# Part of the first modulation vectors computed on TensorE, low parts of the first norm on VectorE, first loads reordered

## The chip, the cores and the metric

One core of a Trainium2 chip runs the whole program. The metric is the device time of one execution in microseconds (us); before the change the median of three runs is 1348.74 us (1347.36 to 1349.37).

## The reference, cut to what matters

The kernel is one inference step of a hybrid encoder layer over 1024 prompt frames and 64 sample frames, model width 1024, all in 32-bit floats. At the start of the layer:

```python
mod = jax.nn.silu(c) @ w_ada + b_ada
sh1, sc1, g1, sh2, sc2, g2 = jnp.split(mod, 6, axis=-1)
h = modulate(rmsnorm(x, ln1), sh1, sc1)        # rmsnorm(x) * g * (1 + sc1) + sh1
rq, rk, rv, rg, aq, ak, av = split_in(h @ w_in)
```

After it come retention and sliding-window attention in four head steps, an output projection, a second norm, a gated MLP with a short convolution, and a final norm. The change touches only what makes `h` and the first products with `w_in`.

## The kernel before, in words

The activations are kept transposed: 8 tiles of 128 model rows (index k) by 1088 frames. Frames are cut into three chunks, c = 0, 1, 2, of 364, 362 and 362 frames; chunk 2 holds the end of the prompt and the sample frames, which have another conditioning vector, so its elementwise operations come in two pieces (298 and 64 frames). A matmul of full accuracy is made as three fp32r passes over a high and a low part of each operand: `act_hl[:, 0]` and `act_hl[:, 1]` for activations, `w_hl` for weights. A high part is written by ScalarE (rounded on the way), a low part is the exact value minus the high part. Weights come in units of 128 output columns; units 0, 1 and 2 are multiplied first.

Every engine runs its own list of instructions in order and waits on semaphores; these lists are written out by hand, and their order is what sets the course of the opening stage:

- SyncE issues the loads in one queue: the conditioning vectors broadcast to all partitions (`silu_c`, 1 MB), modulation tiles of 512 KB (a tile is 128 of the 16x128 scale and shift outputs, outputs on partitions; `load_first_ada`, L495), the three chunks of x (1.4 MB each, `load_x`), weight units, small constants.
- ScalarE applies silu to `silu_c` (L779), squares x (`x_squares`, L755), takes the root of the column sums (`x_root`, L764), splits weights (`split_weights`, L712) and makes high parts, writing the exact value back into a ring of five slots as well (`modulate_x`, L730).
- VectorE multiplies each modulation tile by `silu_c` and sums along the free dimension, once for the prompt and once for the sample (`ada_dots`, L1358, busy on L1368): 14 of the 16 tiles, seven of them ahead of the norm and seven within it. It inverts the roots (`invert`, L1383), adds the bias and makes `scale_n` from a shift and scale pair (`first_vectors(k)`, L1394), and scales x for chunks 1 and 2 (L1425).
- GpSimd multiplies the two other tiles (L1221; ScalarE sums them), multiplies chunk 0 of x by the inverse root (L1230), subtracts the low parts of the weights (L1192) and of all activations (`split_hf`, L1209).
- TensorE sums the squares over partitions with a matrix of ones (L1933, 24 plain fp32 matmuls), then runs the first products k by k: for each k eight groups of three passes, unit u and chunk c, each waiting for the low part of (k, c) (L1963, 192 matmuls). Unit 2 of chunk 2 follows (L1975) with the value transposes between (L1952), and then the head steps (L1918).

Of the kernel before, what the change touches and what calls it, by code (L numbers as in the profile page):

```python
# [19 lines left out]
ALU = mybir.AluOpType  # L20
# [5 lines left out]
P = 128  # L26
# [43 lines left out]
MOD_DVE = (3, 6, 7)  # L70
U_RING = 8
# [33 lines left out]
def hymba_step(nc, x_t, w_units, w_ada, b_ada, cond, gains, conv_wb, conv_st, sinks, ck_t, cv_in, st_in,  # L105
# [4 lines left out]
    with ExitStack() as ctx:  # L110
# [16 lines left out]
        ada_d_phase.close()  # L127
        act_hl = sb("act_hl", [P, 2, KT, T], F32R)
# [91 lines left out]
        X_SQ = [sq[:, 0], sq[:, 1], hf[:, 0], hf[:, 1]]  # L220
        X_SUM_BANK = [0, 1, 2]


        ada_place = [ada_w[:, 0], ada_w[:, 1]] + [t[:, 0:D] for t in (rk, rg, rq, rv, aq)]
        ada_pool_place = [ak[:, 0:D], prob[:].rearrange("p a b c -> p (a b c)")]
# [5 lines left out]
        cond_loaded = sem("cond_loaded")  # L231
        x_loaded = [sem(f"x_loaded{c}") for c in range(3)]
        x_again = [sem(f"x_again{c}") for c in range(3)]
        x_tile_again = sem("x_tile_again")
        ada_loaded = [sem(f"ada_loaded{r}") for r in range(7)]
        ada_pool_loaded = [sem(f"ada_pool_loaded{r}") for r in range(2)]
# [10 lines left out]
        ada_product = sem("ada_product")  # L247
        ada_summed = sem("ada_summed")
# [6 lines left out]
        x_inv_ready = sem("x_inv_ready")  # L255
        x_normed = sem("x_normed")
# [224 lines left out]
        def _(sp):  # L481
# [13 lines left out]
            def load_first_ada(m):  # L495
                if 12 <= m < 14:
                    sp.dma_start(ada_pool_place[m - 12], w_ada[m]).then_inc(ada_pool_loaded[m - 12], 16)
                    return
                nth = ADA_DVE.index(m)
                if nth >= 7:  # L500
                    sp.wait_ge(ada_used, 2 * (nth - 7) + 2)
                sp.dma_start(ada_place[nth % 7], w_ada[m]).then_inc(ada_loaded[nth % 7], 16)
# [25 lines left out]
            load_first_ada(12)  # L528
# [4 lines left out]
            load_first_ada(6)  # L533
            load_unit(1, [1])
            load_unit(2, [2])
            for dst, src in ((b_ada_sb, b_ada), (gains_sb, gains), (ident, ident_in), (conv_wb_sb, conv_wb),
                             (conv_st_sb, conv_st)):
                sp.dma_start(dst[:], src).then_inc(const_loaded, 16)
            for m in (7, 8, 13, 9, 10, 11, 14, 15):
                load_first_ada(m)  # L540
# [163 lines left out]
        def _(act):  # L704
# [25 lines left out]
            def modulate_x(k, c):  # L730

                item = 3 * k + c
                if c == 0:
                    act.wait_ge(vec_ready, k + 1)
                    act.wait_ge(x_normed, k + 1)
                    if item >= 5:
                        act.wait_ge(lo_ready, item - 4)  # L740
                else:
                    act.wait_ge(x_scaled, 2 * k + c)
                for ring in (False, True):
                    for o, tok, m, part in pieces(c):
                        slot = H_RING[item % 5][:, o:o + m]
                        src = xm[:, k, tok:tok + m] if c == 0 else slot
                        ins = act.activation(slot if ring else act_hl[:, 0, k, tok:tok + m], src, ACT.Identity,
                                             bias=mod[:, 2 * k + 1, part:part + 1],
                                             scale=1.0 if c else scale_n[:, 0, k, part:part + 1])
                ins.then_inc(hi_ready, 1)  # L750
# [4 lines left out]
            def x_squares(c):  # L755
                a, n = CHUNKS[c]
                act.wait_ge(x_loaded[c], 16)
                for k in range(KT):
                    item = KT * c + k
                    if item >= 4:  # L760
                        act.wait_ge(sq_used, item - 3)
                    act.activation(X_SQ[item % 4][:, 0:n], xm[:, k, a:a + n], ACT.Square).then_inc(sq_ready, 1)

# [6 lines left out]
            def sum_ada(m):  # L770

                for s in range(2):
                    act.wait_ge(ada_product, 2 * (m - 12) + s + 1)
                    src = ada_pool_place[m - 12] if s else acc[:, 0:D]
                    act.activation(src, src, ACT.Copy, accum_out=mod_part[:, m - 4, s:s + 1]).then_inc(ada_summed, 1)
# [4 lines left out]
            x_squares(0)  # L780
            x_root(0)
            x_squares(1)
            x_root(1)
            x_squares(2)
            split_weights(0, [0])
            x_root(2)
            split_weights(1, [1])
            split_weights(2, [2])
            sum_ada(12)

            act.wait_ge(sq_used, 3 * KT)
            for k in range(KT):
                for c in range(3):
                    modulate_x(k, c)
                if k == 4:
                    sum_ada(13)
# [390 lines left out]
        def _(pool):  # L1187
# [27 lines left out]
            def multiply_ada(m, s):  # L1215

                if s == 0 and m > 12:
                    pool.wait_ge(ada_summed, 2 * (m - 12) - 1)
                pool.wait_ge(ada_pool_loaded[m - 12], 16)
                dst = ada_pool_place[m - 12] if s else acc[:, 0:D]  # L1220
                pool.tensor_tensor(dst, ada_pool_place[m - 12], silu_c[:, s], ALU.mult).then_inc(ada_product, 1)  # L1221

            pool.wait_ge(silu_c_ready, 1)
            for s in range(2):
                multiply_ada(12, s)

            pool.wait_ge(x_inv_ready, 1)
            for k in range(KT):
                x = xm[:, k, 0:CHUNKS[0][1]]
                pool.tensor_tensor(x, x, std[:, 0], ALU.mult).then_inc(x_normed, 1)  # L1230
            for n in range(3):
                split_weights(n, [n])
            for k in range(KT):
                for c in range(3):
                    split_hf(3 * k + c, c, k, H_RING)
                if k in (1, 3):
                    multiply_ada(13, k // 2)
# [106 lines left out]
        def _(dve):  # L1344
# [44 lines left out]
            def first_ada_dots(m):  # L1389

                nth = ADA_DVE.index(m)
                ada_dots(nth, nth // 7 + 1, nth % 7, m % 8 if m < 12 else m - 4)

            def first_vectors(k):  # L1394

                m = 2 * k
                if k < 6:
                    then_wait(add_ada_bias(m, 2, m + 2, m % 8))
                else:
                    dve.wait_ge(ada_summed, 4)  # L1400
                    then_wait(add_ada_bias(m, 2, 12 if k == 6 else len(ADA_DVE), m - 4))
# [3 lines left out]


            dve.wait_ge(silu_c_ready, 1)
            for m in range(7):
                first_ada_dots(m)
                if m in (3, 5):  # L1410
                    invert(m // 2 - 1, m // 2 - 1)
                if m == 3:
                    dve.sem_inc(x_inv_ready, 1)
# [977 lines left out]
```

## Time and profile before

| | us |
|---|---|
| median of 3 runs | 1348.74 |
| the profiled execution | 1349.18 |
| its span, first to last instruction | 1347.4 |
| TensorE busy in it | 1252.2 (93%) |
| VectorE / ScalarE / GpSimd busy | 834.9 / 531.9 / 576.6 |
| mean granted TensorE clock | 0.98 of full |

The profile lists per engine the instructions with start and duration; an operation's duration holds a fixed latency, so that the distance from start to start of a series is what one more operation costs. A granted clock of 1.0 is 2.4 GHz, 0.5 is 1.2 GHz.

### The profile page before, as it was taken

Reading aid. Unit: us, or ns where it says so; the run is one execution under the profiler, and the core shown is the slowest. Engines: PE = TensorE matmul, PEld = TensorE weight load, DVE = VectorE, ACT = ScalarE, POOL = GpSimd, SP = SyncE. Lnnn points to the kernel's source line nnn. Section 1 sums busy time; section 2 is a strip of 40 time slices with the busy share of each in tenths; the row PEclk is TensorE's granted clock in tenths of the full one; section 3 lists DMA queues with packets and bytes.
Section 4 is the critical chain, followed back from the end, with each engine's and each line's share of the span. In section 5 each row is a group of like instructions: output and inputs, shape, how many; then the busy total and the mean of one; then the engine's idle time right before and its main releaser. Section 6 shows DMA issues by size and latency. Waiting matters only on the chain.

```text
span 1347.4 us, 22674 instructions
## 1 busy us (share of the span) xinstructions
PE 1252.2 (93%) x8609; PEld 1193.3 (89%) x8609; DVE 834.9 (62%) x1496; ACT 531.9 (39%) x1074; POOL 576.6 (43%) x351
## 2 busy tenths in 40 slices
PE   5479999999999899778999999999999999999995
PEld 2468898988988899678999999999999999898995
DVE  6966648558376735976566665666656368772305
ACT  5463434344345432444433334333343332424422
POOL 4852113032142342335435344353443577665770
PEclk9799999999999999989999999999999999999998
DMA  9402222223033423212232322323221799595971
GB/s 367 162 35 82 87 73 78 70 88 109 29 115 110 132 68 114 86 45 96 98 113 88 124 97 99 113 88 125 96 99 66 293 353 342 204 334 193 338 257 45
DMA packets 74393, 185.56 MB, mean 138 GB/s; under 512 B 7424, under 2 KB 39744, under 8 KB 74048
## 3 DMA queue, kind: packets, MB, share of 16 engines
q1 hardware_dynamic: 72640, 183.63, 38.0%
q8 instruction: 59, 0.97, 0.3%
q10 hardware_dynamic: 1664, 0.72, 0.2%
q14 instruction: 30, 0.25, 0.1%
HBM read 150.14 MB, written 34.19 MB: 137 GB/s over the span
## 4 chain that ended last, share of the span: by engine, by line
PE 67%; DVE 14%; issue 6%; DMA 5%; POOL 4%; ACT 3%; SPq 0%; DVEq 0%; ACTq 0%; PEldq 0%; POOLq 0%
PE bank L2183 32%; PE bank L1918 13%; PE bank L2223 8%; PE bank L2159 5%; DMA w_raw<-in_w_units 4%; POOL w_more L1331 2%; POOL w_hl L1331 2%; PE bank L2030 2%; DVE ada_out L1368 1%; DVE std L1555 1%; PE bank L2000 1%; PE bank L2015 1%; DMA xm<-in_x_t 1%; PE bank L2064 1%; DVE acc L1825 1%
## 5 line engine op out<-in xcount | busy, mean ns | idle before, releaser
L1918 PE MATMUL bank<-act_hl,w_hl 128*128 128x362 f32 (+1 forms) x1368 | 256.6, 336 | 0.1
L1918 PEld LDWEIGHTS bank<-act_hl,w_hl 128*128 128x128 f32 x1368 | 223.4, 188 | 9.3 <-issue 7.1
L2223 PE MATMUL bank<-u_hl,w_more 128*128 128x362 f32 (+1 forms) x936 | 160.9, 330 | 8.3 <-POOL w_more L1331 7.7
L1192 POOL TENSOR_TENSOR w_hl<-w_raw,w_hl 128x1024 fp32r<-128x1024 f32 x24 | 57.2, 2386 | 260.1 <-ACT w_hl L712 260.1
L2223 PEld LDWEIGHTS bank<-u_hl,w_more 128*128 128x128 f32 x936 | 155.9, 188 | 10.7 <-POOL w_more L1331 9.5
L1331 POOL TENSOR_TENSOR w_more<-w_raw,w_more 128x1024 fp32r<-128x1024 f32 x39 | 109.1, 2816 | 70.9 <-ACT w_more L1093 70.9
L2183 PE MATMUL bank<-x_blocks_b,w_hl 128*128 128x272 f32 x864 | 114.4, 291 | 3.1 <-ACT x_blocks_b L1005 2.0
L2183 PE MATMUL bank<-x_blocks_a,w_hl 128*128 128x272 f32 x864 | 112.9, 289 | 3.9 <-issue 3.9
L2183 PEld LDWEIGHTS bank<-x_blocks_b,w_hl 128*128 128x128 f32 x864 | 111.4, 190 | 4.2 <-ACT x_blocks_b L1005 2.4
L2183 PEld LDWEIGHTS bank<-x_blocks_a,w_hl 128*128 128x128 f32 x864 | 110.4, 189 | 4.4 <-issue 4.3
L2223 PE MATMUL bank<-u_hl,w_hl 128*128 128x362 f32 (+1 forms) x648 | 111.7, 330 | 1.9 <-POOL w_hl L1331 1.9
L2183 PE MATMUL bank<-x_blocks_a,w_ext 128*128 128x272 f32 x840 | 110.1, 290 | 3.6 <-DVE prod_sb L1660 2.4
L2183 PEld LDWEIGHTS bank<-x_blocks_a,w_ext 128*128 128x128 f32 x840 | 107.6, 190 | 4.0 <-issue 2.6
L2223 PEld LDWEIGHTS bank<-u_hl,w_hl 128*128 128x128 f32 x648 | 108.2, 188 | 3.0 <-POOL w_hl L1331 2.5
L2183 PE MATMUL bank<-x_blocks_b,w_ext 128*128 128x272 f32 x840 | 108.3, 287 | 0.0
L2183 PEld LDWEIGHTS bank<-x_blocks_b,w_ext 128*128 128x128 f32 x840 | 106.2, 188 | 0.0
L1295 POOL TENSOR_TENSOR w_ext<-w_raw,w_ext 128x512 fp32r<-128x512 f32 x40 | 53.6, 1349 | 82.5 <-ACT w_ext L982 82.5
L1295 POOL TENSOR_TENSOR w_hl<-w_raw,w_hl 128x512 fp32r<-128x512 f32 x41 | 52.8, 1295 | 79.2 <-ACT w_hl L982 79.2
L1331 POOL TENSOR_TENSOR w_hl<-w_raw,w_hl 128x1024 fp32r<-128x1024 f32 x27 | 73.0, 2719 | 25.7 <-ACT w_hl L1093 25.4
L1093 ACT ACTIVATE w_more<-w_raw 128x1024 fp32r<-128x1024 f32 x39 | 41.3, 1058 | 75.2 <-DMA w_raw<-in_w_units 75.2
L1667 DVE TENSOR_TENSOR up_b<-bank,prod_sb 128x272 f32<-128x272 f32 x44 | 19.4, 441 | 81.2 <-PE bank L2183 81.2
L2159 PE MATMUL bank<-act_hl,w_hl 128*128 128x272 f32 x480 | 64.6, 298 | 4.6 <-POOL w_hl L1288 4.6
(236 smaller groups left out, 2240.7 us busy)
## 6 DMA issues: line engine op xcount, KB each, us to landing
w_raw<-in_w_units SPq DMA_DIRECT2D x142, 512.0 KB, 4.4
ada_w<-in_w_ada_t SPq DMA_DIRECT2D x36, 512.0 KB, 3.7
u_hl<-u_dram SPq DMA_DIRECT2D x44, 362.0 KB, 5.5
u_dram<-acc SPq DMA_DIRECT2D x22, 544.0 KB, 2.7
u_dram<-up_b SPq DMA_DIRECT2D x22, 544.0 KB, 2.7
ada_d<-in_w_ada_t SPq DMA_DIRECT2D x16, 512.0 KB, 5.0
u_hl<-u_dram SPq DMA_DIRECT2D x22, 364.0 KB, 8.2
xm<-in_x_t SPq DMA_DIRECT2D x2, 1448.0 KB, 13.6
```

The costliest lines, as they stand in the source:

```text
L1093: act.activation(w_down(q)[:, 0], w_raw[:, q % 3], ACT.Copy).then_inc(dh_ready, 1)
L1192: pool.tensor_tensor(w_hl[:, slot, 1], w_raw[:, slot], w_hl[:, slot, 0].bitcast(F32), ALU.subtract).then_inc(wl_ready, 1)
L1295: pool.tensor_tensor(w_block(q)[:, 1], a_source(f, i), w_block(q)[:, 0].bitcast(F32), ALU.subtract).then_inc(bl_ready, 1)
L1331: pool.tensor_tensor(w_down(q)[:, 1], w_raw[:, q % 3], w_down(q)[:, 0].bitcast(F32), ALU.subtract).then_inc(dl_ready, 1)
L1368: dve.tensor_tensor_reduce(out, ada_place[place], silu_c[:, s], 1.0, 0.0, ALU.mult, ALU.add, mod_part[:, part, s:s + 1]).then_inc(ada_used, 1)
L1555: dve.reciprocal(std[:, c, 0:n], std[:, c, 0:n]).then_inc(inv_ready, 1)
L1667: ins = dve.tensor_tensor(bb[:, t:t + HC], B[:, 0:HC], gate_sum, ALU.add)
L1918: ins = pe.matmul(bank[c][:, 0:m], w_hl[:, slot, w, k, :], act_hl[:, x, k, a:a + m], start=(pas == 0 and i == 0), stop=(pas == 2 and i == ...
L2030: ins = pe.matmul(bank[6][h, 0:n], av_tok[0:k[1], k[3], h], prob_t[0:k[1], r, g, i, 0:n], start=(i == 0), stop=(i == len(kb) - 1))
L2159: ins = pe.matmul(bank[r % 3][:, 0:HC], w_of[:, w, k, :], act_hl[:, x, k, HC * n:HC * n + HC], start=(pas == i == 0), stop=(pas == 2 and i ...
L2183: ins = pe.matmul(n[:, 0:HC], w_block(q)[:, w, P * k:P * (k + 1)], x_half(h)[:, i, x, k, :], start=(first and pas == k == 0), stop=(pas == ...
L2223: ins = pe.matmul(bank[o][:, 0:m], w_down(q)[:, w, o, :], u_hl[:, q % U_RING, x, 0:m], start=(f == pas == 0), stop=(f == FT - 1 and pas == 2))
```

## The change

Tiles 0 to 9 of the sixteen are no longer multiplied on VectorE (nor 12 and 13 on GpSimd). TensorE transposes each in eight blocks of 128x128 into two PSUM banks, ScalarE copies one bank to SBUF (`w_t`) and VectorE the other, and TensorE multiplies the eight blocks (stationary) by the two columns of `silu_t`, a transposed silu of the conditioning vectors made from a small load. Tiles 10 to 15 stay dots on VectorE, with the old `silu_c`, loaded and activated later. Squares have a buffer of their own, GpSimd adds them in pairs, so TensorE sums 12 arrays in place of 24. VectorE scales all three chunks (GpSimd no longer multiplies chunk 0), ScalarE writes the high part alone, and VectorE makes the low part as (scaled + shift) - high. TensorE starts the first products when the vectors of k = 4 are there. Items (k, c) are taken in a new order, `X_ORDER`.

```diff
+FIRST_COLS = 2 * D + 4 * CHUNKS[0][1] + P + 2 * KT
+PE_ADA = 10
+X_ORDER = ([(0, 0), (1, 0), (2, 0), (0, 1), (1, 1), (2, 1), (3, 0), (3, 1), (0, 2), (1, 2), (2, 2), (3, 2)]
+           + [(k, c) for k in range(4, KT) for c in range(3)])
...
 SP
-            sp.dma_start(silu_c[:, :, :], cond.partition_broadcast(P)).then_inc(cond_loaded, 16)
+            sp.dma_start(ident[:], ident_in).then_inc(ident_loaded, 16)
+            sp.dma_start(cond_rows[0:2 * KT, :], cond.rearrange("s (k p) -> (s k) p", p=P)).then_inc(cond_rows_loaded, 16)
             load_first_ada(0)
             load_first_ada(1)
+            for dst, src in ((b_ada_sb, b_ada), (gains_sb, gains)):
+                sp.dma_start(dst[:], src).then_inc(const_loaded, 16)
             load_x(0)
             load_first_ada(2)
             load_first_ada(3)
             load_x(1)
-            load_first_ada(12)
             load_first_ada(4)
             load_first_ada(5)
             load_x(2)
             load_unit(0, [0])
             load_first_ada(6)
+            load_first_ada(7)
             load_unit(1, [1])
             load_unit(2, [2])
+            load_first_ada(8)
+            load_first_ada(9)
+            sp.dma_start(silu_c[:, :, :], cond.partition_broadcast(P)).then_inc(cond_loaded, 16)
+            for m in range(PE_ADA, 16):
+                load_first_ada(m)
...
 ACT
+            def x_hi_part(k, c):
+                i = X_ORDER.index((k, c))
+                act.wait_ge(x_scaled, i + 1)
+                for o, tok, m, part in pieces(c):
+                    ins = act.activation(act_hl[:, 0, k, tok:tok + m], H_RING[i % 5][:, o:o + m], ACT.Identity,
+                                         bias=mod[:, 2 * k + 1, part:part + 1])
                 ins.then_inc(hi_ready, 1)
...
                     if item >= 4:
-                        act.wait_ge(sq_used, item - 3)
+                        act.wait_ge(sq_used, (item - 4) // 2 + 1)
...
+            def ada_t_copy(t):
+                act.wait_ge(ada_t_done, t + 1)
+                if t >= 2:
+                    act.wait_ge(ada_dot_done, t - 1)
+                act.activation(w_t[:, t % 2, 0:512], bank[2 * (t % 2)][:, :], ACT.Copy).then_inc(ada_t_act, 1)
...
+            act.wait_ge(cond_rows_loaded, 16)
+            act.activation(cond_rows[0:2 * KT, :], cond_rows[0:2 * KT, :], ACT.Silu).then_inc(silu_rows_ready, 1)
+            ada_t_copy(0)
+            ada_t_copy(1)
+            x_squares(0, 0, 8)
+            ada_t_copy(2)
+            ada_t_copy(3)
+            x_root(0)
+            x_hi_part(0, 0)
+            x_hi_part(1, 0)
+            x_squares(1, 0, 4)
+            ada_t_copy(4)
+            x_squares(1, 4, 8)
+            ada_t_copy(5)
+            x_root(1)
+            x_hi_part(2, 0)
+            x_squares(2, 0, 4)
+            for k in range(3):
+                x_hi_part(k, 1)
+            split_weights(0, [0])
+            ada_t_copy(6)
+            x_squares(2, 4, 8)
+            ada_t_copy(7)
+            x_root(2)
+            split_weights(1, [1])
+            x_hi_part(3, 0)
+            x_hi_part(3, 1)
+            split_weights(2, [2])
+            ada_t_copy(8)
+            for k in range(3):
+                x_hi_part(k, 2)
+            ada_t_copy(9)
+            x_hi_part(3, 2)
             act.wait_ge(cond_loaded, 16)
             act.activation(silu_c[:, :, :], silu_c[:, :, :], ACT.Silu).then_inc(silu_c_ready, 1)
+            for k in range(4, KT):
                 for c in range(3):
+                    x_hi_part(k, c)
...
 POOL
+            for p in range(10):
+                add_pair(p)
+            split_weights(0, [0])
+            for p in range(10, 12):
+                add_pair(p)
+            for n in (1, 2):
                 split_weights(n, [n])
-            for k in range(KT):
-                for c in range(3):
-                    split_hf(3 * k + c, c, k, H_RING)
...
 DVE
+            ada_t_copy(0)
+            ada_t_copy(1)
+            first_vectors(0)
+            ada_t_copy(2)
+            ada_t_copy(3)
+            first_vectors(1)
+            invert(0, 0)
+            x_scale((0, 0), (1, 0))
+            x_lo_part((0, 0), (1, 0))
+            ada_t_copy(4)
+            ada_t_copy(5)
+            first_vectors(2)
+            x_scale((2, 0))
+            invert(1, 1)
+            x_lo_part((2, 0))
+            x_scale((0, 1), (1, 1), (2, 1))
+            x_lo_part((0, 1), (1, 1), (2, 1))
+            ada_t_copy(6)
+            ada_t_copy(7)
+            first_vectors(3)
+            x_scale((3, 0), (3, 1))
+            invert(2, 2)
+            x_lo_part((3, 0), (3, 1))
+            x_scale((0, 2), (1, 2), (2, 2))
+            ada_t_copy(8)
+            x_lo_part((0, 2), (1, 2), (2, 2))
+            ada_t_copy(9)
+            x_scale((3, 2))
+            x_lo_part((3, 2))
+            for k in range(4, KT):
+                first_vectors(k)
+                parts = [(k, c) for c in range(3)]
+                x_scale(*parts)
+                if k < KT - 1:
+                    first_ada_dots(2 * k + 2)
+                x_lo_part(*parts)
+                if k < KT - 1:
+                    first_ada_dots(2 * k + 3)
...
 PE
+            def x_sums_of(c, p0, p1):
...
+                if c == 2 and p0 == 0:
+                    pe.wait_ge(std_ready, 1)
+                for p in range(p0, p1):
+                    pe.wait_ge(pair_ready, 4 * c + p + 1)
+                    ins = pe.matmul(bank[X_SUM_BANK[c]][:, 0:n], ones[:, :], x_sq[:, 2 * p % 4, 0:n], start=(p == 0),
+                                    stop=(p == 3))
...
+            ada_transpose(0)
+            ada_transpose(1)
+            ada_dot(0)
+            ada_dot(1)
+            ada_transpose(2)
+            x_sums_of(0, 0, 4)
+            ada_transpose(3)
+            ada_dot(2)
+            ada_dot(3)
+            ada_transpose(4)
+            x_sums_of(1, 0, 2)
+            ada_transpose(5)
+            x_sums_of(1, 2, 4)
+            ada_dot(4)
+            ada_dot(5)
+            x_sums_of(2, 0, 2)
+            ada_transpose(6)
+            ada_transpose(7)
+            x_sums_of(2, 2, 4)
+            ada_dot(6)
+            ada_dot(7)
+            ada_transpose(8)
+            ada_dot(8)
+            ada_transpose(9)
+            ada_dot(9)
+            pe.wait_ge(vec_ready, PE_ADA // 2)
```

## Rows read from the trace of the kernel before

**Rows 1.** The page: two lines of the 40 slices, busy tenths and granted clock.
```profile
PE   5479999999999899778999999999999999999995
...
PEclk9799999999999999989999999999999999999998
```

**Rows 2.** Busy time by stretch: from:to, length, PE, PEld, DVE, ACT, POOL, clock, DMA.
```profile
0.00:46.05 46.05, 17.12 (x48) 9.84 (x49) 34.71 (x35) 23.96 (x41) 26.41 (x20) 0.90 0.98 365
46.05:98.90 52.85, 41.29 (x192) 37.13 (x192) 44.53 (x65) 31.12 (x72) 34.26 (x25) 0.86 0.11 41
...
107.25:1347.40 1240.15, 1187.92 (x8336) 1141.45 (x8336) 753.59 (x1389) 474.48 (x958) 513.60 (x305) 0.99 0.38 134
```

**Rows 3.** The chain that ended last, two pieces of it: start, us, what.
```profile
2.14 10.18 DMA xm<-in_x_t
...
50.42 1.22 DVE ada_out L1368
```

**Rows 4.** Timeline of TensorE, first products: start, us, what, idle before.
```profile
46.05 5.28 PE L1963 MATMUL bank<-act_hl,w_hl 128*128 128x364 f32 x18 [13.66 <-POOL act_hl L1209]
...
62.71 9.47 PE L1963 MATMUL bank<-act_hl,w_hl 128*128 128x364 f32 x42 [3.17 <-POOL act_hl L1209]
...
95.65 3.25 PE L1963 MATMUL bank<-act_hl,w_hl 128*128 128x362 f32 x18 [0.45 <-POOL act_hl L1209]
```

**Rows 5.** Timeline of ScalarE, opening stage and first evacuations.
```profile
19.97 0.56 ACT L767 ACTIVATE std<-bank,eps_sb 128x364 f32<-128x364 f32 x1 [0.73 <-PEq L1937]
20.43 0.89 ACT L762 ACTIVATE sq<-xm 128x362 f32<-128x362 f32 x2
...
45.13 0.60 ACT L747 ACTIVATE act_hl<-hf,mod 128x362 fp32r<-128x362 f32 x1 [1.35 <-DVE hf L1425]
...
97.93 1.20 ACT L802 ACTIVATE rv<-bank 128x364 f32<-128x364 f32 x3 [0.95 <-PE bank L1963]
```

**Rows 6.** Timeline of VectorE: dots, inverse, vectors, scaling, a copy from PSUM.
```profile
8.67 1.23 DVE L1368 CUSTOM_DVE_ANT_0 ada_out<-ada_w,silu_c 128x1024 bf16<-128x1024 f32 x1 [8.67 <-ACT silu_c L779]
...
11.32 1.23 DVE L1368 CUSTOM_DVE_ANT_0 ada_out<-ada_w,silu_c 128x1024 bf16<-128x1024 f32 x1
...
36.92 2.40 DVE L1387 RECIPROCAL std<-std 128x362 f32<-128x362 f32 x1
...
40.16 2.27 DVE L1402 TENSOR_SCALAR scale_n<-mod,gains_sb 128x2 f32<-128x2 f32 x1
...
48.82 0.71 DVE L1425 SCALAR_TENSOR_TENSOR hf<-xm,scale_n,std 128x298 f32<-128x298 f32 x2
...
69.61 0.23 DVE L1402 TENSOR_SCALAR scale_n<-mod,gains_sb 128x2 f32<-128x2 f32 x1
69.87 0.60 DVE L1425 SCALAR_TENSOR_TENSOR sq<-xm,scale_n,std 128x362 f32<-128x362 f32 x1
...
102.94 0.29 DVE L1441 COPY av_tok<-bank 128x128 f32<-128x128 f32 x1 [0.23 <-PE bank L1952]
```

**Rows 7.** Timeline of GpSimd: weight low parts, one activation low part.
```profile
37.76 6.94 POOL L1192 TENSOR_TENSOR w_hl<-w_raw,w_hl 128x1024 fp32r<-128x1024 f32 x3
...
91.29 0.83 POOL L1209 TENSOR_TENSOR act_hl<-hf,act_hl 128x362 fp32r<-128x362 f32 x1 [2.09 <-ACT hf L747]
```

**Rows 8.** TensorE, plain fp32: column sums; loads of a transpose (L2046) and matmul (L2047).
```profile
12.99 2.77 PE L1933 MATMUL bank<-sq,ones 128*128 128x364 f32 x4 [12.99 <-ACT sq L762]
...
17.23 1.39 PE L1933 MATMUL bank<-sq,ones 128*128 128x364 f32 x4
...
168.07 0.14 PEld L2046 LDWEIGHTS bank<-ident,rv 128*128 128x128 f32 x1
168.18 0.30 PEld L2047 LDWEIGHTS bank<-rq,rk 128*128 128x128 f32 x2
```

**Rows 9.** One line's weight loads, windows 46.0:46.25 and 52.3:52.5: ns min/median/max.
```profile
L1963 PEld LDWEIGHTS bank<-act_hl,w_hl x2: 288/313/338, 46.0 to 46.2; 128*128 128x128 f32 x2
...
L1963 PEld LDWEIGHTS bank<-act_hl,w_hl x2: 186/188/189, 52.4 to 52.5; 128*128 128x128 f32 x2
```

More of the change, by code:

```diff
@@ L1213, in _, with add_pair @@
             pool.memset(eps_sb[:, :], EPS).then_inc(pool_const, 1)
[L1215 to L1231, printed above, removed]
[L1232 to L1237 removed]
+            def add_pair(p):
+                n = CHUNKS[p // 4][1]
+                pool.wait_ge(sq_ready, 2 * p + 2)
+                a, b = (x_sq[:, (2 * p + i) % 4, 0:n] for i in range(2))
+                pool.tensor_tensor(a, a, b, ALU.add).then_inc(pair_ready, 1)
+            for p in range(10):
[4 more added lines that the diff above has]
+            for n in (1, 2):
+                split_weights(n, [n])
             for n in (3, 4):
@@ L1428, in _, with x_lo_part @@
                     ins.then_inc(x_scaled, 1)
-                    for tile in ADA_DOTS_IN.get(k, ())[c - 1:c]:
-                        first_ada_dots(tile)
-            dve.sem_inc(ada_used, 4)
-            dve.wait_ge(x_scaled, 2 * KT)
-            dve.wait_ge(x_normed, KT)
+            def x_lo_part(*parts):
+                for k, c in parts:
+                    i = X_ORDER.index((k, c))
+                    dve.wait_ge(hi_ready, i + 1)
+                    for o, tok, m, part in pieces(c):
+                        ins = dve.scalar_tensor_tensor(act_hl[:, 1, k, tok:tok + m], H_RING[i % 5][:, o:o + m],
+                                                       mod[:, 2 * k + 1, part:part + 1],
+                                                       act_hl[:, 0, k, tok:tok + m].bitcast(F32), ALU.add, ALU.subtract)
+                    ins.then_inc(lo_ready, 1)
@@ new lines, in ada_transpose, with ada_dot @@
+            def ada_transpose(t):
+                pe.wait_ge(ada_loaded[t], 16)
+                if t >= 2:
+                    pe.wait_ge(ada_t_act, t - 1)
+                    pe.wait_ge(ada_t_dve, t - 1)
+                for k in range(KT):
+                    ins = pe.transpose(bank[2 * (t % 2) + k // 4][:, P * (k % 4):P * (k % 4) + P],
+                                       ada_place[t][:, P * k:P * k + P], ident[:, :])
+                ins.then_inc(ada_t_done, 1)
+            def ada_dot(t):
+                pe.wait_ge(ada_t_act, t + 1)
+                pe.wait_ge(ada_t_dve, t + 1)
+                if t == 0:
+                    pe.wait_ge(silu_t_ready, 1)
+                if t >= 4:
+                    pe.wait_ge(vec_ready, t // 2 - 1)
+                for k in range(KT):
+                    ins = pe.matmul(bank[6 + t // 2 % 2][:, 2 * (t % 2):2 * (t % 2) + 2], w_t[:, t % 2, P * k:P * k + P],
+                                    silu_t[:, k, :], start=(k == 0), stop=(k == KT - 1))
+                ins.then_inc(ada_dot_done, 1)
@@ L1970, in _ @@
             pe.wait_ge(act_evac, 7)
-            pe.wait_ge(const_loaded, 16 * 5)
+            pe.wait_ge(const_loaded, 16 * 4)
             a, m = CHUNKS[2]
```

160 lines of the change are left out of this document (65 added, 95 removed).

## The prediction, on record before the result

> **What bounds the kernel now.** I read the slices of the page first. TensorE is at 9 tenths in nearly every slice and its clock at full; the gaps lie in slices 1 to 3, the opening [rows 1]. The busy times by stretch then cut the span in three. To 46.05 us the engine does nothing but the 48 records of the column sums. From 46.05 to 98.90 it runs the 192 first products: 41.3 us recorded as busy in 52.9, partly at the lower clock. From 107.25 to the end it is busy 1187.9 of 1240.2 us at clock 0.99 [rows 2]. So the end of the program is the end of the first products plus a stretch that TensorE fills by itself, and nothing of the change lies in that stretch. The whole question is when the first products end: **98.90 us** now (95.65 + 3.25 [rows 4]). The chain of waits says what sets it: the load of x chunk 0 to 12.32, and afterwards VectorE, whose dots stand in it tile after tile [rows 3]. TensorE idles 3.17 us before the matmuls at 62.71, waiting for a low part, and they then run slowly [rows 4].
>
> **Removed.** On VectorE 8.67 to 11.32 are the two dots of one tile, 2.65 us [rows 6]; ten tiles less is 26.5 us. GpSimd loses 24 low parts of 0.83 us or more [rows 7], the scaling of chunk 0 and four products; TensorE 12 of 24 column sums; ScalarE the 24 write-backs. The load of silu_c, 1 MB, leaves the head of the queue: the first 3.6 MB had landed at 12.32 us [rows 3], some 0.39 MB per us after a start at 3.1, so x(0) should land near 9.9, x(1) near 16.4, x(2) near 22.9, tile 9 near 32.3.
>
> **Added, by the piece.** VectorE: a scale or low part costs 0.50 us by the start-to-start distance behind a duration of 0.60, and 0.68 for chunk 2's two pieces (0.71 recorded) [rows 6]. All 24 low parts and 8 scales of chunk 0 are 13.4 + 4 us. An inverse stays 2.45, a pair of small vector operations 0.4 [rows 6]. A copy of 128 columns from PSUM took 0.29 [rows 6]; for 512 I take 0.7 (bounds 0.4 and 1.2, four times the row), ten are 7. So VectorE's balance is about zero. ScalarE: a PSUM copy of 512 columns 0.5, from three of 364 in 1.20; a square 0.39, a root 0.46 plus a table load, a high part 0.50 [rows 5]. GpSimd: a pair of squares added 0.85, like a low part, and a weight low part 2.3 (three in 6.94) [rows 7]. TensorE at 2.4 GHz: a column sum of two records 0.61 (17.23: four in 1.39, 0.305 apart) and twice that at 1.2 GHz (12.99: four in 2.77) [rows 8]. Transposes and fp32 weight loads follow each other 0.11 us apart [rows 8], so eight transposes are 0.88. The multiplication by two columns isn't shown anywhere; it is 8 fp32 matmuls, each two weight loads of 128 columns and two matmuls of nearly nothing. Bounds per load are 0.055 (only half of that distance) and 0.19, a load's whole duration with nothing hidden [rows 9]. I take 0.11, the distance of fp32 loads: 16 x 0.11 = **1.76 us** a tile. At 1.2 GHz a load's duration goes from 0.19 to 0.34 [rows 9]; I take twice the price, 3.5.
>
> By the Trainium skill, page "TensorE: Matmul & The Clock Gate", section "LDWEIGHTS (loading the stationary operand)", a load takes its columns over 1.2 GHz, which makes 1.7 us a tile at either clock. The rows speak against it at the lower clock, where the load lengthens by 0.15 us; by the rule the cold case below would be some 13 us milder.
>
> **The schedule.** What counts is not the sums but the order of the four lists, where a hand-off goes round TensorE, ScalarE, GpSimd and VectorE. Walking the new lists with these prices at 2.4 GHz:
> - x(0) at 9.9: squares in a ring of four, 0.39 each, pairs of 0.85, sums of 0.61, and about 0.3 us from a sum's end to ScalarE. Sums done at 16.9.
> - Transpose 3, dots 2 and 3 stand behind these sums: 16.9 + 0.9 + 3.5 + 0.4 = 21.8. Then VectorE's vectors 0.4 and inverse 2.45, scales at 24.6 to 25.6. ScalarE has high parts (0,0) and (1,0) ahead of the squares of chunk 1, so these, whose data came at 16.4, start at 26.3.
> - Squares, pairs and sums of chunk 1 with transpose 5 between: done 32.8. Dots 4 and 5, which stand behind them: vectors(2) at 36.8. Scale (2,0) and its high part let the squares of chunk 2 start at 38.4; VectorE is in the second inverse until 40.2.
> - Two sums, transposes 6 and 7 to 43.4. ScalarE waits for three scales of chunk 1, splits weights, copies, and squares the rest at 45.1; GpSimd has the split of unit 0 (2.3) ahead of the last two pairs. Sums done 49.8, dots 6 and 7 until 53.3, vectors(3) at 53.9.
> - Two scales, third inverse to 57.8. GpSimd's split of unit 2 runs 57.1 to 59.4 and holds VectorE, as the three splits held a 0.23 us operation for 2.27 (40.16) [rows 6, 7]. Low parts, scales of chunk 2 until 62.5; only then copy 8, dot 8 (to 65.0), transpose 9, copy 9, dot 9 (to 68.8), vectors(4): **69.7**. There the first products start, 23.7 us later than now.
> - 192 passes at 0.165 us (18 in 3.25 [rows 4]) are 31.7: 101.4. VectorE per k: 0.4 + 1.7 + 2.65 + 1.7 + 2.65 = 9.1, three times, plus 1.3 for the late silu_c, plus 3.9: last low part at 100.6, and most of k = 7 behind it: **104**.
>
> So the backlog of four k removes the idle time of the products (52.9 us now, 34 then) but not the 23.7 us of late start; 104 - 98.9 is +5.
>
> **The clock.** This schedule has TensorE idle in the opening for 6, 4 and 9 us. After 3.17 us of idling the 42 matmuls at 62.71 took 9.47 us where 42 x 0.165 + 0.3 is 7.2; after 13.66 us, 18 took 5.28 and not 3.3 [rows 4]. So part of the opening runs at 1.2 GHz. If all did, the chain gets longer by 8 dots of 1.75, some 6 transposes of 0.9 and 12 sums of 0.61: about 26 us. I take a third, +8.
>
> **Sum.** The profiled execution took 1349.18 (span 1347.4 and 1.8 around it), 0.4 over the median of three, within their spread. 1349.2 + 5 + 8 = **1362 us**.
>
> **Rivals.**
> - *TensorE stays at 2.4 GHz* in spite of the gaps: 1354. For it: the sums before, with idle times around 1 us, kept it. Chance 0.20.
> - *TensorE is at 1.2 GHz nearly throughout*, since most of its new work is short: 1349.2 + 5 + 26 = 1380. Against it: stretches of 6 to 9 us with work back to back. Chance 0.20.
> - *Faster.* The hand-offs overlap more than I walked, above all if the chain from vectors(1) over the inverse and the two high parts to the squares of chunk 1 is not waited for long. With nothing but loads and own work VectorE would have some 29 us before tile 9, whose dot would end at 32.3 + 0.9 + 0.7 + 1.8 + 0.5, near 36.5; the products would start there and end with VectorE at 36.5 + 31 + 3.5 = 71: 1322. It becomes faster than now where vectors(4) comes before 64.7 at full clock. Each of the five detours is in the lists, so only a part can be saved: 1340. Chance 0.10.
> - *No change*: dots at 0.055 us a load save 8 x 0.9 = 7 us of the walk at most, which ends at 99 with a full clock: 1350. Chance 0.05.
>
> The forecast, a partly slow opening, has 0.45.
>
> **Numbers.** 0.2% is 2.7 us, about what a measurement of this kernel can tell from no change. The range 1352 to 1381 takes in the forecast, both clock cases and the dear bounds of copy and dot; it leaves out faster and same and a little above. Faster 0.10, same 0.05, slower 0.85.
>
> **What would show it.** First L1963-like product near 78 (70 to 96) and not before 46; last low part near 108; sums of the three chunks done near 18, 36 and 55, each followed by two dots; ScalarE idle for VectorE's scales before the squares of chunks 1 and 2; granted clock near 0.5 behind TensorE's gaps; after the products the same 1248 us as before. The prediction is wrong if the products start before 60, if a tile's 16 loads take under 1 us or over 4, or if the later stretch changes its length.

## The result and the profile after

The changed kernel takes **1372.51 us** (median of 4 runs, 1368.9 to 1375.29) against 1348.05 for the kernel before on the same chip (4 runs, 1347.34 to 1349.37): ratio 1.0175, 95% interval 1.0159 to 1.0190. The profiled execution took 1373.15 (span 1371.1). The forecast was 1362, with a range of 1352 to 1381, and slower with 0.85.

Two lines of the page, busy tenths and granted clock in 40 slices of 34.3 us. The first two slices of TensorE are fuller than in [rows 1], and its clock in slices 2 and 3 is lower.
```profile
PE   7779999999999999877999999999999999999995
...
PEclk9569999999999999989999999999999999999998
```

Busy time of each engine by stretch; columns are from:to, length, PE, PEld, DVE, ACT, POOL (each with the number of its instructions), clock, DMA share, GB/s. The stretches are the opening, the first products, and the rest of the program.
```profile
0.00:87.90 87.90, 61.58 (x266) 51.26 (x266) 31.99 (x57) 33.03 (x61) 18.68 (x21) 0.70 0.54 203
87.90:122.27 34.37, 34.37 (x192) 34.07 (x192) 28.97 (x62) 10.23 (x24) 0.00 (x0) 0.93 0.10 34
...
130.78:1371.00 1240.22, 1191.37 (x8336) 1144.87 (x8336) 753.78 (x1389) 474.53 (x958) 512.16 (x305) 0.98 0.38 134
```
Against [rows 2]: the last stretch has 1240.2 us as before. The products need 34.4 us instead of 52.9 and have no gap. But they begin at 87.90 instead of 46.05 and end at 122.27 instead of 98.90. These **23.4 us** are all but 0.6 of the 24.0 by which the two profiled executions differ. In the opening VectorE is busy for 32 of 88 us, ScalarE for 33, TensorE for 62 at a clock of 0.70. That mean is too high: the view gives 1.00 for all of the first 27 us, yet the multiplications at 8.73 below take the time that they take under 0.50 at 61.45. For this part I go by durations.

The timeline of TensorE in the opening (start, us, what, idle before it) shows the chain:
```profile
8.73 6.83 PE L2023 MATMUL bank<-silu_t,w_t 128*128 128x2 f32 x32
...
20.60 2.80 PE L1996 MATMUL bank<-x_sq,ones 128*128 128x364 f32 x4 [0.81 <-POOL x_sq L1243]
23.70 1.59 PE L2010 MATMUL bank<-ident,rg 128*128 128x128 f32 x8 [0.30 <-PE bank L1996]
25.12 4.02 PE L2023 MATMUL bank<-silu_t,w_t 128*128 128x2 f32 x32
29.00 1.95 PE L2010 MATMUL bank<-ident,rq 128*128 128x128 f32 x8
35.78 2.78 PE L1996 MATMUL bank<-x_sq,ones 128*128 128x362 f32 x4 [4.83 <-POOL x_sq L1243]
...
40.06 2.27 PE L1996 MATMUL bank<-x_sq,ones 128*128 128x362 f32 x4
42.64 4.57 PE L2023 MATMUL bank<-silu_t,w_t 128*128 128x2 f32 x32 [0.30 <-PE bank L1996]
50.96 2.75 PE L1996 MATMUL bank<-x_sq,ones 128*128 128x362 f32 x4 [3.75 <-POOL x_sq L1243]
...
58.62 2.53 PE L1996 MATMUL bank<-x_sq,ones 128*128 128x362 f32 x4 [2.22 <-POOL x_sq L1243]
61.45 6.96 PE L2023 MATMUL bank<-silu_t,w_t 128*128 128x2 f32 x32 [0.30 <-PE bank L1996]
...
77.59 3.54 PE L2023 MATMUL bank<-silu_t,w_t 128*128 128x2 f32 x16 [7.37 <-issue]
...
83.77 3.54 PE L2023 MATMUL bank<-silu_t,w_t 128*128 128x2 f32 x16 [0.83 <-ACT w_t L774]
87.90 34.37 PE L2082 MATMUL bank<-act_hl,w_hl 128*128 128x364 f32 x192 [0.59 <-DVE scale_n L1420]
```
An fp32 matmul leaves two records, its halves, so a tile's eight matmuls are x16. L2023 is the multiplication by two columns: two tiles take 6.96 us at 61.45, where the granted clock is 0.50, and 4.02 at 25.12. L1996 are column sums: four records take 2.78 at 35.78, against 1.39 in [rows 8]. The idle times ahead of them are waits for GpSimd's pairs. Those at 35.78 and 50.96 waited for ScalarE's squares, which stand behind high parts; those at 58.62 for GpSimd's own weight split (55.30 to 57.67). ScalarE:
```profile
32.80 1.11 ACT L753 ACTIVATE act_hl<-hf,mod 128x364 fp32r<-128x364 f32 x2 [5.01 <-DVE hf L1438]
33.82 1.67 ACT L767 ACTIVATE x_sq<-xm 128x362 f32<-128x362 f32 x4
...
48.41 0.60 ACT L753 ACTIVATE act_hl<-hf,mod 128x364 fp32r<-128x364 f32 x1 [5.38 <-DVE hf L1438]
48.91 1.67 ACT L767 ACTIVATE x_sq<-xm 128x362 f32<-128x362 f32 x4
```
It is idle for 5.0 and 5.4 us until VectorE's scales come, and squares right after.

The opening varies from one execution to the next. In two later ones with the same opening (the two-column run and its control below) the products begin at 91.29 and 88.11; the first of them has tiles 2 and 3 at 6.83 us where 4.02 stand above. A start that differs by 3 us says nothing yet.

### The profile page after: what moved, and what is told of

It reads as the page before. It is cut to its first block, busy times and chain, and to the rows that moved or that the text cites. A ratio compares the mean times of both kernels' runs of the same rounds, so it can differ in the third digit from the quotient of the medians.

```text
span 1371.1 us, 23098 instructions
## 1 busy us (share of the span) xinstructions
PE 1293.1 (94%) x8826; PEld 1235.0 (90%) x8826; DVE 816.8 (60%) x1515; ACT 520.4 (38%) x1046; POOL 533.2 (39%) x327
## 4 chain that ended last, share of the span: by engine, by line
PE 72%; DVE 10%; issue 5%; DMA 5%; POOL 5%; ACT 3%; SPq 0%; DVEq 0%; ACTq 0%; POOLq 0%
PE bank L2302 31%; PE bank L1980 13%; PE bank L2342 8%; PE bank L2278 5%; DMA w_raw<-in_w_units 3%; PE bank L2082 2%; POOL w_more L1345 2%; PE bank L2023 2%; POOL w_hl L1345 2%; PE bank L2149 1%; DVE std L1617 1%; PE bank L2119 1%; PE bank L2134 1%; PE bank L1996 1%; PE bank L2010 1%
## 5 line engine op out<-in xcount | busy, mean ns | idle before, releaser
L1980 PEld LDWEIGHTS bank<-act_hl,w_hl 128*128 128x128 f32 x1368 | 223.3, 188 | 9.3 <-issue 7.1
L1345 POOL TENSOR_TENSOR w_more<-w_raw,w_more 128x1024 fp32r<-128x1024 f32 x39 | 109.0, 2814 | 69.7 <-ACT w_more L1116 69.7
L2278 PEld LDWEIGHTS bank<-act_hl,w_hl 128*128 128x128 f32 x480 | 64.3, 199 | 4.9 <-POOL w_hl L1302 4.8
```

What stands on the lines that cost most here:

```text
L1345: pool.tensor_tensor(w_down(q)[:, 1], w_raw[:, q % 3], w_down(q)[:, 0].bitcast(F32), ALU.subtract).then_inc(dl_ready, 1)
L1980: ins = pe.matmul(bank[c][:, 0:m], w_hl[:, slot, w, k, :], act_hl[:, x, k, a:a + m], start=(pas == 0 and i == 0), stop=(pas == 2 and i == ...
L2278: ins = pe.matmul(bank[r % 3][:, 0:HC], w_of[:, w, k, :], act_hl[:, x, k, HC * n:HC * n + HC], start=(pas == i == 0), stop=(pas == 2 and i ...
```

## The experiments

Three theories. **Hand-offs and slow clock:** the products start late because the opening is one chain through four engines, whose TensorE pieces run partly at 1.2 GHz. **Too much TensorE work:** the transposes and multiplications would be late in any order. **VectorE:** its work in all, with the low parts added, sets the end. The kernel before was timed again beside each group of runs, with medians of 1348.4 to 1349.8 us.

**Only the multiplications shortened.** The kernel leaves out seven of the eight blocks of each sum, so its modulation vectors are not the layer's.
```
-                for k in range(KT):
+                for k in range(1):
                     ins = pe.matmul(bank[6 + t // 2 % 2][...], w_t[...], silu_t[:, k, :], ...
```


> The changed kernel with each tile's multiplication cut to one of its eight blocks, so that the modulation vectors of tiles 0 to 9 are sums over 128 of 1024 inputs. It leaves 14 of 16 weight loads out. Theory H: eight tiles' multiplications (2 to 9) are on the chain, 3.5 us each at 1.2 GHz, so 8 x 3.0 = 24 us less if the clock stays as it is: products start at 62 to 68, time 1347 to 1353. Rival: the multiplications hide beside ScalarE's and VectorE's waits, and little changes: 1368 to 1373.

1351.15 us (10 runs), ratio 1.0020 [1.0011, 1.0030]. TensorE's timeline:
```profile
30.31 2.78 PE L1996 MATMUL bank<-x_sq,ones 128*128 128x362 f32 x4 [6.52 <-POOL x_sq L1243]
...
69.22 34.74 PE L2082 MATMUL bank<-act_hl,w_hl 128*128 128x364 f32 x192 [1.93 <-DVE scale_n L1420]
```
The products start 18.7 us earlier, yet end at 103.96, 5 behind [rows 4]. So even with seven eighths of the multiplications free this order of hand-offs gains nothing over the kernel before, and the sums at 30.31 still take the price of 1.2 GHz behind 6.5 us of waiting. The start is 1.2 us above the range that I expected: with the multiplications nearly gone, 23 of the 42 us of late start are still there.

**Only the gaps filled.** Thirty multiplications that nobody reads keep TensorE busy where it would wait.
```
+            def filler(times):
+                for _ in range(times):
+                    pe.matmul(bank[2][:, 0:364], ones[:, :], xm[:, 0, 0:364], start=True, stop=True)
...
             ada_transpose(4)
+            filler(7)
...
             ada_dot(5)
+            filler(5)
             x_sums_of(2, 0, 2)
             ada_transpose(6)
+            filler(6)
             ada_transpose(7)
...
             ada_transpose(8)
+            filler(12)
```


> The changed kernel with 30 more column-sum matmuls (0.61 us each at 2.4 GHz) put where TensorE waits: 7 behind transpose 4, 5 behind dot 5, 6 behind transpose 6, 12 behind transpose 8. They compute nothing that is used. Theory H (the late start of the products is a chain of hand-offs whose TensorE pieces run at 1.2 GHz because of the waits between them): the clock stays at full, the pieces of the chain halve, the products start at 70 to 74 us in place of 87.9, time 1355 to 1360. Rival W (TensorE simply has too much work in the opening, whatever the clock does): more work makes it later, 1373 to 1390.

1365.44 us (4 runs), ratio 1.0124 [1.0107, 1.0141]: *more* work on TensorE makes the kernel 7 us faster than the changed one. The profiled execution was the fastest of the four, 1360.95 beside 1365.1 to 1366.5. Its timeline:
```profile
54.75 4.26 PE L2023 MATMUL bank<-silu_t,w_t 128*128 128x2 f32 x32 [0.30 <-PE bank L1996]
58.87 1.95 PE L2010 MATMUL bank<-ident,prob 128*128 128x128 f32 x8
60.61 9.46 PE L2030 MATMUL bank<-xm,ones 128*128 128x364 f32 x24
69.91 1.84 PE L2023 MATMUL bank<-silu_t,w_t 128*128 128x2 f32 x16
...
76.48 34.37 PE L2091 MATMUL bank<-act_hl,w_hl 128*128 128x364 f32 x192 [0.59 <-DVE scale_n L1420]
```
The start falls from 87.90 to 76.48; I had expected 70 to 74. Not all of the 11.4 us are the fillers': in this execution tiles 0 and 1 took 4.08 us instead of 6.83, and the sums of chunk 0 ended at 20.79 instead of 23.40, both ahead of the first filler. That leaves 8.8 at most, and the medians say 7. The pieces behind the fillers did get shorter (tiles 6 and 7 take 4.26 for 6.96), so the clock is a cause. What is missing shows at 58.87: these transposes follow two tiles of multiplications without any idle time, and take 1.95 us, the slow price. The idle gaps were not all that slowed the clock.

**What the two-column multiplication does to the clock.** In the changed kernel, behind the first products, where the clock is at full, a run without a wait:
```
+            for _ in range(64):
+                pe.matmul(bank[1][:, 0:2], ones[:, :], xm[:, 0, 0:2], start=True, stop=True)
             pe.wait_ge(act_evac, 9)
```


> The kernel after with 64 more multiplications of two moving columns, back to back and without a wait, behind the transposes of the values after the first products, where TensorE has run at full clock for 40 us. If the clock falls only with idle time, they take 64 x 0.25 = 16 us at full clock and the time is 1373 + 16 = 1389. If it falls in such a run of two-column multiplications though TensorE is never idle, their rate drops from 0.125 to 0.217 us for each half within the run, they take 22 to 28 us, and the matmuls behind them begin at 1.2 GHz: 1395 to 1403.

1401.47 us, a single execution. Windows (same columns as above) and then TensorE's timeline:
```profile
133.60:136.00 2.40, 2.40 (x24) 2.40 (x23) 0.28 (x1) 0.00 (x0) 0.00 (x0) 1.00 0.00 0
136.00:138.00 2.00, 2.00 (x14) 2.00 (x14) 0.00 (x0) 0.00 (x0) 0.00 (x0) 0.66 0.00 0
138.00:158.00 20.00, 20.00 (x96) 20.00 (x95) 0.00 (x0) 0.00 (x0) 0.00 (x0) 0.50 0.00 1
```
```profile
133.59 24.53 PE L2101 MATMUL bank<-xm,ones 128*128 128x2 f32 x128
157.98 2.77 PE L1980 MATMUL bank<-act_hl,w_hl 128*128 128x364 f32 x8
```
With TensorE busy every moment the granted clock went to 0.50 and stayed there; eight matmuls behind it took 2.77 us, where the changed kernel has 1.59 at that point. The products began late in this execution, at 91.29, which is 3.4 of the 29 us that it is slower than the changed kernel.

**The control with a full width.** The same 64 with 364 moving columns.


> The control of the run with 64 two-column multiplications: the same 64 in the same place with 364 moving columns. At full clock throughout a half takes about 0.152 us (12 fillers' rate), 128 x 0.152 = 19.5 us, so the time is 1373 + 17 = 1390 to 1393, less than with two columns, and the granted clock stays 1.00 in the stretch and the matmuls behind it take 0.165 each. If mere repetition of one multiplication lowers the clock, it is over 0.50 for the same 20 us and the time is above 1405.

1408.65 us, a single execution; windows of two stretches, and the timeline:
```profile
140.00:145.00 5.00, 5.00 (x18) 3.15 (x17) 0.00 (x0) 0.00 (x0) 0.00 (x0) 1.00 0.00 0
...
155.00:160.00 5.00, 5.00 (x18) 3.14 (x17) 0.00 (x0) 0.00 (x0) 0.00 (x0) 1.00 0.02 3
```
```profile
130.44 39.31 PE L2101 MATMUL bank<-xm,ones 128*128 128x364 f32 x128
169.31 1.78 PE L1980 MATMUL bank<-act_hl,w_hl 128*128 128x364 f32 x8
```
My price was wrong by two: 39.31 / 128 is 0.307 us a half, the 0.305 of the column sums (the prediction had it, the expectation halved it). By the time alone I would have called the clock down, as the expectation's last sentence has it; the granted clock is 1.00 throughout and the matmuls behind it take 1.78. So it is neither the repetition nor the short gaps ahead of the run, which both have; the kernels differ in nothing but the width of the multiplication. Each stands on one execution.

**Only the order of two lists.** ScalarE squares ahead of the high parts it would wait for; GpSimd adds all pairs before it splits weights.
```
+            x_squares(1, 0, 4)
             x_hi_part(0, 0)
             x_hi_part(1, 0)
-            x_squares(1, 0, 4)
...
-            x_hi_part(2, 0)
             x_squares(2, 0, 4)
+            x_hi_part(2, 0)
...
-            split_weights(0, [0])
             ada_t_copy(6)
             x_squares(2, 4, 8)
             ada_t_copy(7)
+            split_weights(0, [0])
...
-            for p in range(10):
+            for p in range(12):
                 add_pair(p)
```


> The changed kernel with another order of its lists only: ScalarE squares half a chunk before the high parts that wait for VectorE's scales (chunks 1 and 2), the first weight split goes behind the squares, and GpSimd adds all pairs before the first weight low part. No work is added or taken. Theory H: two of the detours go, 4 to 6.5 us, products start at 82 to 84 and the time is 1366 to 1369. Rival W (TensorE's own work is the bound): 1372 to 1374, no change.

1365.59 us (4 runs), ratio 1.0122 [1.0105, 1.0139]; the products start at 82.31. Start and time are about as expected: some 5.6 us of the chain were two lists written in the wrong order.

**Both at once**, the order and the fillers.


> Both edits on the kernel after at once: squares and pairs ahead of what waits, and the thirty filler multiplications in TensorE's gaps. If the late start is the hand-offs and the slow clock together, the products start at 71 to 74 (87.9 less 11.4 for the fillers and 5.6 for the order, but not below the 69.7 of the working at full clock), and the time is 1354 to 1359. If the two hide each other it is that of the fillers alone, 1361 to 1367. In no case does it fall to the kernel before, since VectorE's second phase is untouched.

1361.88 us (4 runs), ratio 1.0092 [1.0069, 1.0115]. Against the changed kernel the medians fell by 7.1 us with the fillers, 6.9 with the order and 10.6 with both. Whether the gains add is not decided: the time lies in the range that I gave for gains that hide each other, yet 3.6 us under the fillers alone, and the two intervals overlap. The start, 76.55, equals the 76.48 of the fillers alone, but both executions were ahead before any filler, here by 3.8 us (sums of chunk 0 done at 19.57). VectorE's timeline there shows what else the start waits for:
```profile
64.40 2.54 DVE L1446 SCALAR_TENSOR_TENSOR act_hl<-hf,mod,act_hl 128x364 fp32r<-128x364 f32 x2
66.86 1.35 DVE L1435 SCALAR_TENSOR_TENSOR sq<-xm,scale_n,std 128x298 f32<-128x298 f32 x4
68.14 0.71 DVE L1435 SCALAR_TENSOR_TENSOR hf<-xm,scale_n,std 128x298 f32<-128x298 f32 x2
68.77 0.68 DVE L1426 COPY w_t<-bank 128x512 f32<-128x512 f32 x1
```
The copy that tile 8's multiplication needs ends at 69.45; the last fillers end at 69.7, the multiplication starts at 69.58. Both stand in the way, and I didn't separate them: a run with fewer fillers at the end was not made.

**Does a late start cost by itself?** In the kernel *before*, one more wait ahead of the products.
```
+            pe.wait_ge(vec_ready, 4)
             pe.wait_ge(wl_ready, 3)
```


> The kernel before with one wait more: the first products wait for the vectors of k = 3, some 64 us in place of 46. Theory H says that a late start costs nothing while the last low part comes late enough: 64 + 32 to 34 is 96 to 98, beside a last low part at 95.6, so the products end at 98 to 100 and the time is 1347 to 1350. Rival (a late start is paid in full or in good part, since the low parts then wait for nothing but the products pile up): 1352 to 1366.

1349.17 us (10 runs), ratio 0.9999 [0.9989, 1.0008].
```profile
63.89 31.44 PE L1964 MATMUL bank<-act_hl,w_hl 128*128 128x364 f32 x174 [30.87 <-DVE scale_n L1402]
95.77 3.26 PE L1964 MATMUL bank<-act_hl,w_hl 128*128 128x362 f32 x18 [0.45 <-POOL act_hl L1209]
```
TensorE begins 17.8 us later and ends at 99.03 instead of 98.90, since the last low part is what it waits for. The prediction's threshold for "faster", vectors(4) before 64.7, is of the right size: up to about there a late start is free in that kernel.

**Fewer tiles on TensorE.** Six and four of the sixteen, the others dotted by VectorE in the idle time of its opening.
```
-PE_ADA = 10
+PE_ADA = 6
-X_ORDER = ([(0, 0), (1, 0), (2, 0), (0, 1), ...
+X_ORDER = [(0, 0), (0, 1), (1, 0), (1, 1), (0, 2), ...
...
+            sp.dma_start(silu_c[:, :, :], cond.partition_broadcast(P)).then_inc(cond_loaded, 16)
...
             load_x(0)
+            load_first_ada(6)
+            load_first_ada(7)
...
             ada_t_copy(1)
             first_vectors(0)
+            first_ada_dots(6)
+            first_ada_dots(7)
...
-            pe.wait_ge(vec_ready, PE_ADA // 2)
+            pe.wait_ge(vec_ready, 3)
```


> Six tiles stay on TensorE (0 to 5), the other ten are dotted on VectorE, those of tiles 6 to 10 in the opening, where the kernel after left VectorE idle for most of the first 60 us; squares and sums do not stand behind hand-offs, the loads are reordered for it, the products wait for three pairs of vectors instead of five. Late start (hand-offs and slow clock): with fewer TensorE pieces in the chain the products' end is set by the last low part again, worked out at 84 to 90 with about 9.1 us for each k in the second phase less the dots that are gone from it, so products end at 88 to 93 and the time is 1338 to 1345, faster than before. TensorE has too much work whatever the order: at six tenths of the work the products start at 65 to 70 and the time is 1345 to 1352. The rest of the change (VectorE's low parts) is what costs: end of products over 105, 1355 or more.

> Like the kernel with six tiles, but with four on TensorE and twelve on VectorE. Late start by hand-offs: the last low part moves by the two dots that VectorE has more (2 x 2.3 us) against six tiles, so products end at 91 to 96 and the time is 1341 to 1348, behind six tiles by 3 to 5. Too much TensorE work: four tiles are better than six, by 3 us or more.

Six: 1349.14 us, ratio 0.9992 [0.9982, 1.0001]. Four: 1351.38, ratio 1.0012 [1.0002, 1.0021]. Both missed my range. The order of the two is the one I expected, with 2.2 us between them instead of 3 to 5, so TensorE's work as such is not what holds the kernel back. (The six-tile time alone would also fit that rival, 1345 to 1352, but its start does not: 57.35 and not 65 to 70.) Windows of the six-tile kernel and then its timeline of TensorE:
```profile
60.00:70.00 10.00, 10.00 (x54) 10.00 (x53) 9.79 (x24) 5.42 (x12) 0.00 (x0) 0.86 0.01 2
70.00:80.00 10.00, 10.00 (x63) 10.00 (x62) 9.65 (x22) 1.89 (x4) 0.00 (x0) 1.00 0.00 0
80.00:90.00 10.00, 8.15 (x48) 7.56 (x46) 9.64 (x20) 1.89 (x4) 0.00 (x0) 1.00 0.01 2
```
```profile
57.35 26.57 PE L2157 MATMUL bank<-act_hl,w_hl 128*128 128x364 f32 x144 [0.59 <-DVE scale_n L1459]
85.08 4.23 PE L2157 MATMUL bank<-act_hl,w_hl 128*128 128x364 f32 x24 [1.16 <-DVE act_hl L1488]
94.06 5.58 PE L2157 MATMUL bank<-act_hl,w_hl 128*128 128x364 f32 x24 [4.74 <-DVE act_hl L1488]
```
The start is now early enough, at 57.35, and TensorE waits 4.74 us for VectorE's low part at the end; VectorE is busy 9.6 to 9.8 in 10 us. The four-tile kernel has such waits of 4.39, 4.30 and 2.35 us and ends its products at 102.16. In the six-tile one the last low part starts at 94.42; my estimate of 84 to 90 took no time for GpSimd holding VectorE. VectorE's timeline has equal halves of a dot, held during a weight split of GpSimd (48.22 to 51.42) and free:
```profile
49.26 3.24 DVE L1421 CUSTOM_DVE_ANT_0 prob_t<-prob_t,silu_c 128x1024 f32<-128x1024 f32 x1
...
72.08 1.23 DVE L1421 CUSTOM_DVE_ANT_0 ada_w<-ada_w,silu_c 128x1024 f32<-128x1024 f32 x1
```
With two scales in 3.84 us at 42.21 (free 1.1) and a small operation in 0.91 at 41.27 (free 0.23) the holds from 41 us on make 5.4 us of the 4.4 to 10.4 by which I missed.

**The version that beats both.** Six tiles, with VectorE's dots moved into its remaining idle time and tile 10 loaded earlier.
```
             ada_t_copy(1)
+            first_ada_dots(6)
             first_vectors(0)
-            first_ada_dots(6)
             first_ada_dots(7)
+            first_ada_dots(8)
             ada_t_copy(2)
...
-            first_ada_dots(10)
             ada_t_copy(5)
+            first_ada_dots(11)
```


> The kernel with six tiles, with VectorE's dots one step earlier: tile 6 ahead of the first vectors, tile 8 ahead of the second copy, and so on, tile 11 in the opening too; tile 10 is loaded ahead of the three units. In the six-tile run VectorE worked from 58 to 94.4 us without a gap and set the products' end at 99.64, while it still sat idle 6.0, 2.8 and 2.2 us before 33. If VectorE's total is what binds there, some 5 us of these are filled, the last low part starts at 88 to 91 instead of 94.4, the products end at 93 to 97 and the time is 1342 to 1347, 0.2 to 0.5% under before. If it is TensorE (its start at 57.4 plus 192 passes), nothing moves: 1348 to 1351.

**1345.0 us** (9 runs, 1342.98 to 1347.26; before 1348.37), ratio 0.9975 [0.9966, 0.9985]. Windows of its two stretches and TensorE's timeline:
```profile
0.00:54.60 54.60, 39.20 (x169) 30.55 (x169) 40.21 (x51) 25.25 (x45) 22.78 (x21) 0.88 0.87 327
54.60:94.58 39.98, 35.46 (x192) 34.86 (x192) 34.14 (x80) 15.11 (x36) 0.00 (x0) 0.91 0.09 30
```
```profile
88.77 5.81 PE L2157 MATMUL bank<-act_hl,w_hl 128*128 128x364 f32 x24 [4.52 <-DVE act_hl L1488]
```
The products end at 94.58, 5.1 before the six-tile kernel's and 4.3 before [rows 4]. Only VectorE's list and the loads moved, and the time followed, within the range expected: with six tiles VectorE's total binds.

## Why the prediction was right in its sign and 10 us off in its size

- **What bounds, and the later stretch.** Right: 1240.2 us before and after, and the time follows the products' end: from there to the end of the span are 1247.9 to 1249.0 us in every run but the one with shortened multiplications (1246.6) and the two with 64 multiplications inserted.
- **Structure of the walk.** Right in order, and in size with some luck. The last low part comes 29.5 us behind the start (117.39 on VectorE), the walk had 30.9; a k took 8.7 us (vectors at 96.12, 104.84, 113.55) and not 9.1; start to end of the products is 34.4, the walk had 34.3. But the reason is another: in the walk TensorE needs 31.7 and waits for the last low parts; in the run it never waits within the 192 products, and is slower itself (0.50 over the first 3.1 us, 1.00 only from 95.0, 0.93 in all). And the walk's own terms, 27.3 + 1.3 + 3.9, make 32.5 and not 30.9, so its +5 should have been near +7. The split of unit 2 did hold VectorE at 72.44, as foreseen.
- **VectorE's balance.** The "ten tiles less" forget that tiles 12 and 13 came to VectorE: 14 tiles before, 6 after, so eight less and 21.2 us instead of 26.5. The walk counts the dots one by one, so the forecast doesn't hang on it. VectorE's busy time did not stay but fell by 18.1 us, from 834.9 to 816.8; among what went are the holds of the kernel before, where half a dot took 2.44 us at 23.25 and not 1.23. In the rival "no change", 104 less 7 is 97 and not 99.
- **The multiplication's price, seen nowhere before.** Right at both ends: 1.71 us a tile at full clock (in the six-tile run a tile's starts at 37.76 and what follows it at 39.47), 3.41 at 1.2 GHz (two tiles from 61.45 to 68.27), for 1.76 and 3.5.
- **Copies from PSUM.** 0.69 on VectorE and 0.60 on ScalarE, for 0.7 and 0.5; adding a pair of squares took 0.95, not 0.85. These are small.
- **The clock term is the step that was mis-sized.** "I take a third, +8." The walk at full clock had the start at 69.7, the run at 87.90: +18.2, 70% of the 26 of the all-cold case. Step by step the measured chain falls behind the walk: sums of the three chunks done at 23.4, 42.3 and 61.2 for 16.9, 32.8 and 49.8 (6.5, 9.5, 11.4 late), products 18.2 late. Not quite all of it is the clock: x(0) came at 11.2 and not at 9.9. With 18.2 in place of 8 the sum is 1349.2 + 5 + 18 = 1372, against 1373.15, the 5 being right by the luck named above. The ten tiles' 160 records fill 29.5 us where the prediction's prices make 17.6 at full clock and 35 at 1.2 GHz: most of them were slow.
- **Why a third was too little.** The first 6.5 us were lost before any gap that I counted: TensorE's first instruction is at 4.72, and the multiplications of tiles 0 and 1 took 6.83 us at 8.73, for the 3.5 of the walk. After that I counted idle gaps alone, and argued against the rival of a nearly all-slow clock with "stretches of 6 to 9 us with work back to back". These stretches were largely two-column multiplications, and the two-column run shows that such a stretch lowers the clock by itself. What the transposes between them do to it was not tested. By the rows the truth lay between my forecast and that rival.
- **The clock is a cause, but not all.** The fillers took at most 8.8 us off the start and 7 off the time by removing gaps; the order of two lists took 5.6 and 6.9.
- **The rival "faster"** asked for fewer detours in the chain. With this split of ten tiles no run reached it; with six and VectorE's idle time used it came, by 3.4 us.
- **The price of weight loads.** The changed kernel's loads for L2023 took 0.333 us in the slow stretch from 61.4, and those of the last kernel mostly 0.192 in a stretch whose granted clock averaged 0.93. The trace gives them as count, then ns min/median/max, the changed kernel first:
```profile
L2023 PEld LDWEIGHTS bank<-silu_t,w_t x32: 285/333/333, 61.4 to 68.0; 128*128 128x128 f32 x32
```
```profile
L2099 PEld LDWEIGHTS bank<-silu_t,w_t x15: 190/192/333, 39.6 to 41.2; 128*128 128x128 f32 x15
```
The Trainium skill, "TensorE: Matmul & The Clock Gate", section "LDWEIGHTS (loading the stationary operand)", gives a load as its columns over 1.2 GHz, with no term for the clock. For these fp32 loads the measurement decides against reading it as one price for both clocks, and twice the price was rightly taken at 1.2 GHz.

## What to carry to other kernels

Before moving a small product to TensorE, walk the hand-offs rather than summing the engines: the change took eight tiles' dots, some 21 us, off VectorE and put ten tiles in a chain in which every engine waits for the next. Price its pieces at 1.2 GHz if they are mostly weight loads with a few moving columns, even where they stand back to back. Then choose the split by which list becomes full: with ten tiles the chain was the bound, with four and six VectorE was, and six with VectorE's idle time filled beat the kernel before by 0.25%.

## What the runs showed of the hardware that I had not expected

- TensorE's granted clock went from 1.00 to 0.50 within a run of 128 two-column halves without any idle time, and 64 multiplications of 364 columns in the same place kept it at 1.00. At the low clock a half takes 0.21 us (96 in 20.0) instead of 0.10 (24 in 2.40). Both rest on one execution each.
- Work that nobody reads can pay: 30 extra multiplications made the changed kernel 7 us faster.
- Where GpSimd split weights, half a VectorE dot took 3.24 us instead of 1.23, and two scales, with a pair of squares added behind the split, 3.84 where two take 1.1. GpSimd pays too: its split beside that dot took 3.20 us, against 2.35 for the one ahead of it.
- The printed granted clock was 1.00 in the first 27 us of the changed kernel while two tiles took 6.83 us, the price under 0.50.
